# Two-layer hybrid encoder with a hierarchical MoE on one core: gate and up of each layer's first batch run together by parts, and the units that follow are loaded by parts

## The chip, the core and the metric

One core of one Trainium2 chip runs the whole program. The metric is the device time of one execution in microseconds (us). The engines that matter are TensorE (PE, with its weight loads PEld), VectorE (DVE), ScalarE (ACT), and SyncE (SP), which here only issues the DMAs that bring the weights from HBM. 16 DMA engines move the bytes.

## The reference, cut to what matters

Two layers over 256 tokens of width 1024 in float32. Each has a mixer (attention) and then a mixture of experts: 4 groups of 8 experts, the best group and its best two experts for each token.

```
for layer in range(DEPTH):                    # 2
    x = x + mixer(rmsnorm(x))                 # attention, w_in and w_out
    h = rmsnorm(x)
    pg = softmax(h @ wg + bg); g_idx = argmax(pg)
    ...                                       # top 2 of the 8 experts in the group -> comb
    for g in range(MOE_GROUPS):               # 4
        a = einsum('nd,edf->nef', h, w_gate[g])      # 8 experts, d = 1024, f = 256
        u = einsum('nd,edf->nef', h, w_up[g])
        act = silu(a) * u * comb[:, g, :, None]
        y = y + einsum('nef,efd->nd', act, w_down[g])
    x = x + y
```

## The kernel before

**Weights.** All 32 experts of a layer are loaded, 3 matrices each (gate, up, down), every matrix one *unit* of 128 partitions x 2048 floats (8 KB a partition, 1 MB). Each layer has 96 such units beside those of its mixer. A ring of 19 buffers, and 6 more that other tensors give up in the course of a layer, hold them. `place_units` fixes which buffer unit n takes (`WHERE[n]`: buffer, how many loads it has had, the unit that it replaces). SP issues the loads in the order of n: `load(n, src)` waits until PE has used the unit that lay there (`s_used`) and issues one DMA. One waiting load holds back all behind it.

**Experts.** The experts run in 8 *batches* of 4 (`batch`, on PE, ACT and DVE). Each expert takes 32 slots of the 128 columns. A batch on PE: gather the tokens of its slots (`gather`, one-hot matrices made on DVE), the gate products over the 8 chunks c of d (`rows_of(0, c)`: 4 matmuls of 256 columns, one for each expert), the up products (`rows_of(1, c)`), two transposes of the product silu(gate) * up and two of the scatter weights, the down products, and the scatter into the residual. Gate results lie in PSUM bank 4, up results in bank 0. ACT makes the silu (L1324) when gate is done, DVE multiplies it with up (L1708) when up is done. The records count two matmuls for each `pe.matmul` of float32.

**The first batch of a layer** follows the router. Before it the ring is full of weights and PE has freed nothing for a while, so nothing is left to load. It is cut finer: the tokens are gathered in four quarters (`gather_two(q)`, 2 chunks each, into the banks in `FIRST_BANK`), DVE copies each quarter out (L1659, `s_first`), and the gate products start on the first quarter. The four gate units of this batch are `PARTED`: the units that replace them (k = 25 to 28 of the layer's 96) are each loaded by three DMAs (`load_part`), of 512, 512 and 1024 columns (`PART_ENDS`: 2 KB, 2 KB and 4 KB a partition). The first two wait for `s_part`, which PE raises after chunks 0 and 1 and after chunks 2 and 3; the last waits for `s_used`. The four up units are given back together when up is done, and what replaces them (k = 29 to 32) comes in whole units.

Lines: L1048 gather matmuls of the first batch, L1056 gate and up matmuls, L1112 down, L1122 scatter, L653 a whole-unit load, L662 a load of a part.

Of the kernel before, what the change touches and what calls it, by code (L numbers as in the profile page):

```python
# [16 lines left out]
NT = SEQ // P  # L17
NC = D // P
# [8 lines left out]
DFF = 256  # L27
# [12 lines left out]
STAGE = BATCH  # L40
# [85 lines left out]
def first_unit(layer, part):  # L126
    at = 0 if layer == 0 else SLABS[0] + OUTS + PER_ROUND
    return at + {"in": 0, "out": SLABS[layer], "experts": SLABS[layer] + OUTS}[part]
# [1 line left out]

UNITS = first_unit(1, "experts") + PER_ROUND

PARTED = [first_unit(l, "experts") + j for l in range(2) for j in range(STAGE)]
PART_ENDS = (UNIT // 4, UNIT // 2, UNIT)

HALVED = [first_unit(l, "experts") + PER_ROUND - 1 for l in range(2)]
# [34 lines left out]
def hybrid_moe_kernel(nc, xT_d, small_d, bias_d, rope_d, ab_in, ab_out, c_in, c_out, gate_d, up_d, down_d, out_d):  # L171
    with ExitStack() as ctx:
# [28 lines left out]
        place = sb("place", [P, NT, 8], U32)  # L201
# [99 lines left out]
        UP_BANK = [0, 4, 3, 0]  # L301


        FIRST_BANK = [(2, 0), (3, 0), (0, 0), (2, 1)]


        Y = [6, 7, 5, 1]
# [9 lines left out]
        s_part = sem("first_parts_used")  # L317
# [85 lines left out]
        class Main:  # L403


            sig, slot = main, slot_main
# [208 lines left out]
        def _(sp):  # L615
# [39 lines left out]
            def load_part(n, src, part):  # L655
                s, _, was = WHERE[n]
                cols = slice((0, *PART_ENDS)[part], PART_ENDS[part])
                if part < len(PART_ENDS) - 1:
                    sp.wait_ge(s_part, (len(PART_ENDS) - 1) * (n >= first_unit(1, "in")) + part + 1)
                else:  # L660
                    sp.wait_ge(s_used, was + 1)
                sp.dma_start(ring_of(n)[:, cols], src[:, cols]).then_inc(s_unit[s], 16)  # L662

            for layer in range(2):
                if layer:
                    sp.wait_ge(s_used, 1 + max(n for n in range(first_unit(1, "in")) if LOW <= WHERE[n][0] < INPUT))
                    sp.dma_start(rope_all, rope_d[:, :]).then_inc(s_rope, 16)
                for s in range(layer == 0, SLABS[layer]):
                    load(first_unit(layer, "in") + s, (ab_in, c_in)[layer][s])
                    if layer == 0 and s == 2:  # L670
                        sp.dma_start(small[:, S_FIRST:S_ALL], small_d[:, S_FIRST:S_ALL]).then_inc(s_small, 16)
                        for u in extra.unit:
                            sp.sem_inc(u, 16)
                for s in range(OUTS):
                    load(first_unit(layer, "out") + s, (ab_out, c_out)[layer][s])
                weights = (gate_d, up_d, down_d)

                def expert_unit(k):
                    return weights[k % PER_BATCH // STAGE][layer, BATCH * (k // PER_BATCH) + k % STAGE]

                def load_round(rd):
                    sp.wait_ge(extra.used, EXTRA_RING * rd.turns)
                    for k in range(PER_ROUND):
                        if k >= EXTRA_RING:
                            sp.wait_ge(extra.used, EXTRA_RING * rd.turns + k - EXTRA_RING + 1)
                        e = BATCH * (k // PER_BATCH) + k % STAGE
                        sp.dma_start(low[k % EXTRA_RING][:, :], weights[k % PER_BATCH // STAGE][layer, e])\
                            .then_inc(extra.unit[k % EXTRA_RING], 16)

                for k in range(PER_ROUND):  # L690
                    if k == PER_BATCH * BEFORE_EXTRA:
                        extra_rounds(sp, layer, load_round, [(u, 16 * PER_ROUND // EXTRA_RING) for u in extra.unit])
                    n = first_unit(layer, "experts") + k
                    if WHERE[n][2] in PARTED:
                        if WHERE[n][2] == first_unit(layer, "experts"):
                            for part in range(len(PART_ENDS)):
                                for j in range(STAGE):
                                    load_part(n + j, expert_unit(k + j), part)
                        continue
                    load(n, expert_unit(k))  # L700
# [42 lines left out]
        def _(pe):  # L743
# [278 lines left out]
            def batch(rd, step, place):  # L1022
# [15 lines left out]
                    if t == NT - 1:  # L1038
                        ins.then_inc(sig.gather_ps, 1)

                def gather_two(q, *tiles):
                    for t in tiles or range(NT):
                        if q == 0:
                            pe.wait_ge(sig.onehot, NT * g + t + 1)
                        b, half = FIRST_BANK[q]
                        for c in range(2):
                            at = (2 * q + c) * P
                            ins = pe.matmul(bank2(b, 4)[:, 2 * half + c, :], tokens[:, t, at:at + P], onehot[:, t, :],  # L1048
                                            start=(t == 0 and c == 0), stop=(t == NT - 1), skip_group_check=True)
                    if t == NT - 1:  # L1050
                        ins.then_inc(s_first_ps, 1)

                def rows_of(stage, c):
                    for j in range(BATCH):
                        w = rd.weights(place, stage, j).rearrange("p (c n) -> p c n", c=NC)
                        ins = pe.matmul(bank((4, 0)[stage])[j * SLOTS:(j + 1) * SLOTS, 0:DFF],  # L1056
                                        gathered[:, c, j * SLOTS:(j + 1) * SLOTS], w[:, c, :],
                                        start=(c == 0), stop=(c == NC - 1))
                    return ins

                first = sig is main and place == 0
                if first:
                    gather_two(0)
                    gather_two(1, 0)
                else:
                    for half, t in ((0, 0), (0, 1), (1, 0), (1, 1)):
                        gather(half, t)
# [1 line left out]
                after(pe, sig.scatter, g)  # L1069
                after(pe, sig.hidden, g)  # L1070
                rd.arrived(pe, step, place, 0)
                for c in range(NC):
                    if first and c % 2 == 0:
                        pe.wait_ge(s_first, 4 * rd.layer + c // 2 + 1)
                    elif c % 4 == 0:
                        pe.wait_ge(sig.gather, 2 * g + c // 4 + 1)
                    ins = rows_of(0, c)
                    if first and (c + 1) * DFF in PART_ENDS[:-1]:
                        ins.then_inc(s_part, 1)
                    if first and c == 1:  # L1080
                        gather_two(1, 1)
                        gather_two(2)
                    elif first and c == 3:
                        gather_two(3)
                ins.then_inc(sig.used, STAGE)
                if first:
                    pe.sem_inc(sig.gather_ps, 2)
                if not last:
                    rd.arrived(pe, step, place, 1)
                    for c in range(NC):  # L1090
                        ins = rows_of(1, c)
                    ins.then_inc(sig.used, STAGE)

                if last:
                    turn_scatter(rd.layer, g)
# [719 lines left out]
```

## Time and profile before

| | |
|---|---|
| median of 3 runs | 640.93 us (640.05 to 643.5) |
| profiled execution, its span | 639.0 us |
| PE busy | 571.4 us (89%) |
| moved by DMA | 233.60 MB, mean 366 GB/s |

The span is that of one profiled execution from its first instruction to its last, 1.9 us below the median of the timed runs; the profile gives no other time for that execution. A PE that is busy 89% of the time does not mean that PE sets the time everywhere: the page shows the DMA engines at nine tenths and more in about two thirds of the slices.

### The profile page before, as it was taken

The numbers are of one execution on the slowest core, as the hardware profiler recorded it, in microseconds if no ns is written. First come the engines' busy times: TensorE is split into PE (matmuls) and PEld (weight loads), VectorE is DVE, ScalarE is ACT, GpSimd is POOL, SyncE is SP. The second block draws the span as 40 slices with busy tenths as digits, with TensorE's granted clock in tenths as the row PEclk, the third lists the DMA queues.
The fourth block names the chain that finished last, engine by engine and source line by source line (L and its number), as shares of the span: only waits on it lengthen the run. The fifth ranks groups of instructions, "written<-read, shape, count | busy, mean of one in ns | idle before, by whom it ended". The sixth has DMA issues, their size and how long they took to land.

```text
span 639.0 us, 12022 instructions
## 1 busy us (share of the span) xinstructions
PE 571.4 (89%) x4984; PEld 410.2 (64%) x4984; DVE 215.8 (34%) x723; ACT 139.6 (22%) x359; POOL 6.1 (1%) x25
## 2 busy tenths in 40 slices
PE   8999999999999698676999999999999968868696
PEld 8888776885566365352768876788556636535273
DVE  4243446163232122020426687406323212202041
ACT  3143455231101000000131366613110100000011
POOL 0100000000000000000010000000000000000000
PEclk9999999999999989797999999999999998969799
DMA  8999946579999999999999992456999999999994
GB/s 327 422 419 420 419 143 232 222 275 349 422 419 421 417 421 419 421 420 422 419 417 419 419 421 112 196 198 267 346 421 420 421 418 419 419 422 421 421 421 193
DMA packets 36782, 233.60 MB, mean 366 GB/s; under 512 B 4080, under 2 KB 4208, under 8 KB 10608
## 3 DMA queue, kind: packets, MB, share of 16 engines
q1 hardware_dynamic: 34992, 227.49, 87.4%
q10 hardware_dynamic: 1728, 5.24, 2.2%
q8 instruction: 44, 0.72, 0.5%
q14 instruction: 18, 0.15, 0.1%
HBM read 231.67 MB, written 1.05 MB: 364 GB/s over the span
## 4 chain that ended last, share of the span: by engine, by line
PE 67%; DMA 20%; SPq 6%; DVE 4%; ACT 2%; issue 1%; DVEq 0%; ACTq 0%
PE banks L786 14%; PE banks L1056 12%; DMA xT<-in_moe_w_up 9%; DMA ring<-in_moe_w_down 9%; PE banks L872 7%; PE banks L1112 7%; SPq L653 5%; PE banks L1122 5%; PE banks L1035 4%; PE banks L832 2%; PE banks L849 2%; PE banks L860 2%; DMA ring<-in_ab_w_in 2%; PE banks L996 1%; PE banks L986 1%
## 5 line engine op out<-in xcount | busy, mean ns | idle before, releaser
L1056 PE MATMUL banks<-ring,desk 128*32 128x256 f32 x1472 | 111.8, 383 | 16.1 <-DMA xT<-in_moe_w_up 9.0
L786 PE MATMUL banks<-ring,hT 128*128 128x256 f32 x416 | 94.6, 382 | 0.1
L1056 PEld LDWEIGHTS banks<-ring,desk 128*32 128x32 f32 x1472 | 59.5, 110 | 46.6 <-issue 20.4
L786 PEld LDWEIGHTS banks<-ring,hT 128*128 128x128 f32 x416 | 77.3, 190 | 13.3 <-issue 3.6
L1112 PE MATMUL banks<-ring,desk 128*32 128x512 f32 x384 | 60.3, 691 | 21.7 <-DMA ring<-in_moe_w_down 10.2
L1035 PE MATMUL banks<-desk,hT 128*128 128x128 f32 x448 | 55.7, 285 | 10.4 <-issue 10.4
L1035 PEld LDWEIGHTS banks<-desk,hT 128*128 128x128 f32 x448 | 55.3, 202 | 11.8 <-issue 11.2
L872 PE MATMUL banks<-heads,ring 128*128 128x256 f32 x256 | 61.9, 387 | 0.1
L872 PEld LDWEIGHTS banks<-heads,ring 128*128 128x128 f32 x256 | 46.4, 190 | 12.6 <-issue 6.9
L1056 PE MATMUL banks<-shared,desk 128*32 128x256 f32 x288 | 53.9, 408 | 0.0
L1122 PEld LDWEIGHTS banks<-desk 128*128 128x128 f32 x224 | 41.4, 190 | 17.0 <-issue 11.9
L1122 PE MATMUL banks<-desk 128*128 128x256 f32 x224 | 52.1, 386 | 0.0
L1112 PEld LDWEIGHTS banks<-ring,desk 128*32 128x32 f32 x384 | 15.3, 124 | 56.9 <-issue 49.8
L1324 ACT ACTIVATE desk<-banks 128x256 f32<-128x256 f32 x16 | 6.1, 384 | 184.6 <-PE banks L1056 184.6
L1667 DVE TENSOR_TENSOR desk<-banks,small 128x512 f32<-128x512 f32 x28 | 19.4, 692 | 76.1 <-PE banks L1035 76.1
L1710 DVE COPY desk<-banks 128x512 f32<-128x512 f32 x14 | 9.7, 692 | 92.9 <-PE banks L1112 92.9
L1708 DVE TENSOR_TENSOR desk<-banks,desk 128x256 f32<-128x256 f32 x14 | 5.9, 425 | 84.0 <-PE banks L1056 84.0
L1056 PEld LDWEIGHTS banks<-shared,desk 128*32 128x32 f32 x288 | 25.4, 117 | 8.1
L1112 PE MATMUL banks<-shared,desk 128*32 128x512 f32 x48 | 25.8, 687 | 0.0
L1056 PE MATMUL banks<-xT,desk 128*32 128x256 f32 x96 | 25.1, 422 | 0.0
L1523 DVE CUSTOM_DVE_ANT_0 shared<-banks,desk 128x256 f32<-128x256 f32 x32 | 12.6, 423 | 35.1 <-PE banks L832 27.8
L1329 ACT ACTIVATE desk<-banks 128x256 f32<-128x256 f32 x14 | 5.4, 384 | 76.0 <-PE banks L1103 76.0
(191 smaller groups left out, 655.6 us busy)
## 6 DMA issues: line engine op xcount, KB each, us to landing
ring<-in_moe_w_down SPq DMA_DIRECT2D x54, 1024.0 KB, 27.0
ring<-in_moe_w_gate SPq DMA_DIRECT2D x46, 1024.0 KB, 26.9
ring<-in_moe_w_up SPq DMA_DIRECT2D x46, 1024.0 KB, 26.9
shared<-in_moe_w_up SPq DMA_DIRECT2D x10, 1024.0 KB, 20.2
ring<-in_ab_w_in SPq DMA_DIRECT2D x8, 1024.0 KB, 18.7
shared<-in_moe_w_gate SPq DMA_DIRECT2D x8, 1024.0 KB, 15.0
xT<-in_moe_w_up SPq DMA_DIRECT2D x6, 1024.0 KB, 22.3
shared<-in_moe_w_down SPq DMA_DIRECT2D x6, 1024.0 KB, 26.3
```

What stands on the lines that cost most here:

```text
L653: sp.dma_start(ring_of(n), src).then_inc(s_unit[s], 16)
L786: ins = pe.matmul(bank2(SLAB_BANK[layer][s], NT)[:, t, :], hT[:, c, t * P:(t + 1) * P], w[:, c, :], start=(c == 0 and t == 0), stop=(c == ...
L832: ins = pe.matmul(bank2(r, NT)[:, t, :], heads[rows, i, t * P:(t + 1) * P], keysT[rows, kt, :], start=(t == 0), stop=True, skip_group_chec ...
L849: ins = pe.transpose(bank2(2 + r, NT)[:, c, t * P:(t + 1) * P], prob[:, r, t, c * P:(c + 1) * P], ident)
L860: ins = pe.matmul(bank(4)[r * HD:(r + 1) * HD, 0:SEQ], values[layer][:, c, cols[r]:cols[r] + HD], probT_of(layer, i)[:, r, c, :], start=(c ...
L872: ins = pe.matmul(bank2(Y[cp], 2)[:, c % 2, :], w[:, k % 2, c * P:(c + 1) * P], attT[:, k, :], start=False, stop=(k == PAIRS - 1 and c % 2 ...
L1035: ins = pe.matmul(bank(2 + half)[:, c * P:(c + 1) * P], tokens[:, t, half * HALF + c * P:half * HALF + (c + 1) * P], onehot[:, t, :], star ...
L1056: ins = pe.matmul(bank((4, 0)[stage])[j * SLOTS:(j + 1) * SLOTS, 0:DFF], gathered[:, c, j * SLOTS:(j + 1) * SLOTS], w[:, c, :], start=(c = ...
L1112: ins = pe.matmul(bank(2 + half)[j * SLOTS:(j + 1) * SLOTS, :], hiddenT[:, k, j * SLOTS:(j + 1) * SLOTS], w[:, k, half * HALF:(half + 1) * ...
L1122: ins = pe.matmul(bank2(Y[c // 2], 2)[:, c % 2, :], outputs[:, c * P:(c + 1) * P], scatter, start=False, stop=(c % 2 == 1), skip_group_che ...
L1523: ins = V.tensor_tensor_reduce(score[:, b, t, :], bank2(b, NT)[:, t, :], bias[:, b, t, :], 1.0, 3.0e38, ALU.add, ALU.min, negmax[:, b, t:t ...
L1667: V.tensor_tensor(gathered[:, 4 * h:4 * h + 4, :], bank2(2 + h, 4), gains[:, 2 * rd.layer + 1, 4 * h:4 * h + 4].unsqueeze(2) .to_broadcast ...
```

## The change

The first batch of each layer runs on PE by parts: chunks 0 and 1 of gate, then of up; then a gather; chunks 2 and 3 of gate, then of up; a gather; chunks 4 to 7 of gate, then of up. Both tiles of the second quarter are now gathered ahead of the first gate product. `s_part` is raised after each of gate and up. Eight units instead of four are `PARTED`, so k = 25 to 32 are each loaded by three DMAs, in the order: first part of all eight, second part of all eight, last part of all eight. Two quarters of the gathered tokens get other places in PSUM, since bank 0 now holds up results.

```diff
-PARTED = [first_unit(l, "experts") + j for l in range(2) for j in range(STAGE)]
+PARTED = [first_unit(l, "experts") + j for l in range(2) for j in range(2 * STAGE)]
...
-        FIRST_BANK = [(2, 0), (3, 0), (0, 0), (2, 1)]
+        FIRST_BANK = [(2, 0), (3, 0), (2, 1), (3, 1)]
...
-                    sp.wait_ge(s_part, (len(PART_ENDS) - 1) * (n >= first_unit(1, "in")) + part + 1)
+                    layer, stage = int(n >= first_unit(1, "in")), PARTED.index(was) // STAGE % 2
+                    sp.wait_ge(s_part, 2 * ((len(PART_ENDS) - 1) * layer + part) + stage + 1)
...
                             for part in range(len(PART_ENDS)):
-                                for j in range(STAGE):
+                                for j in range(2 * STAGE):
                                     load_part(n + j, expert_unit(k + j), part)
...
                 if first:
                     gather_two(0)
-                    gather_two(1, 0)
+                    gather_two(1)
...
-                for c in range(NC):
-                    if first and c % 2 == 0:
-                        pe.wait_ge(s_first, 4 * rd.layer + c // 2 + 1)
-                    elif c % 4 == 0:
-                        pe.wait_ge(sig.gather, 2 * g + c // 4 + 1)
-                    ins = rows_of(0, c)
-                    if first and (c + 1) * DFF in PART_ENDS[:-1]:
-                        ins.then_inc(s_part, 1)
-                    if first and c == 1:
-                        gather_two(1, 1)
-                        gather_two(2)
-                    elif first and c == 3:
-                        gather_two(3)
-                ins.then_inc(sig.used, STAGE)
                 if first:
+                    rd.arrived(pe, step, place, 1)
+                    for part, (begin_c, end_c) in enumerate(((0, 2), (2, 4), (4, NC))):
+                        for stage in range(2):
+                            for c in range(begin_c, end_c):
+                                if stage == 0 and c % 2 == 0:
+                                    pe.wait_ge(s_first, 4 * rd.layer + c // 2 + 1)
+                                ins = rows_of(stage, c)
+                            if part < len(PART_ENDS) - 1:
+                                ins.then_inc(s_part, 1)
+                            else:
+                                ins.then_inc(sig.used, STAGE)
+                        if part < len(PART_ENDS) - 1:
+                            gather_two(2 + part)
                     pe.sem_inc(sig.gather_ps, 2)
```

PE at the first batch of layer 0, before: the gather (L1048) of the first quarter and half of the second, then gate (L1056) and gathers in turn, and up in one piece at the end. In brackets stand the semaphores that a row waits for; `first_inputs_ready` is a quarter that DVE has copied out.

```order
L1048 MATMUL banks<-desk,hT 128x128 x3
L1056 MATMUL banks<-ring,desk 32x256 [waits unit_loaded15,unit_loaded16,unit_loaded14,first_inputs_ready,unit_loaded13,largest_count_ready]
L1056 MATMUL banks<-ring,desk 32x256 x7
L1048 MATMUL banks<-desk,hT 128x128 x6
L1056 MATMUL banks<-ring,desk 32x256 [waits first_inputs_ready]
...
L1048 MATMUL banks<-desk,hT 128x128 x4
L1056 MATMUL banks<-ring,desk 32x256 [waits first_inputs_ready]
...
L1056 MATMUL banks<-ring,desk 32x256 [waits unit_loaded0,unit_loaded1,unit_loaded18,unit_loaded17]
L1056 MATMUL banks<-ring,desk 32x256 x31
```

The same place in the changed kernel, whose lines stand one further down:

```order
L1049 MATMUL banks<-desk,hT 128x128 x5
L1057 MATMUL banks<-ring,desk 32x256 [waits unit_loaded17,unit_loaded18,unit_loaded16,unit_loaded0,unit_loaded15,unit_loaded1,unit_loaded14,first_inputs_ready,unit_loaded13,largest_count_ready]
L1057 MATMUL banks<-ring,desk 32x256 x15
L1049 MATMUL banks<-desk,hT 128x128 x4
L1057 MATMUL banks<-ring,desk 32x256 [waits first_inputs_ready]
L1057 MATMUL banks<-ring,desk 32x256 x15
L1049 MATMUL banks<-desk,hT 128x128 x4
L1057 MATMUL banks<-ring,desk 32x256 [waits first_inputs_ready]
...
L1057 MATMUL banks<-ring,desk 32x256 [waits first_inputs_ready]
L1057 MATMUL banks<-ring,desk 32x256 x23
```

The number of matmuls is the same. Two gather matmuls moved ahead of the first gate product, each run of gate products is followed by one of up products, and gate is complete 8 + 8 matmuls later in the row than before.

SP's queue behind the last load that doesn't need the first batch, before:

```order
L653 DMA shared<-in_moe_w_gate 128x2048 [waits logits_in_psum]
L662 DMA ring<-in_moe_w_gate 128x512 [waits first_parts_used] x3
L662 DMA ring<-in_moe_w_up 128x512 [waits first_parts_used]
L662 DMA ring<-in_moe_w_gate 128x512 [waits first_parts_used] x3
L662 DMA ring<-in_moe_w_up 128x512 [waits first_parts_used]
L662 DMA ring<-in_moe_w_gate 128x1024 [waits units_used] x3
L662 DMA ring<-in_moe_w_up 128x1024 [waits units_used]
L653 DMA ring<-in_moe_w_up 128x2048 [waits units_used] x3
L653 DMA ring<-in_moe_w_down 128x2048 [waits units_used] x4
```

And in the changed kernel:

```order
L653 DMA shared<-in_moe_w_gate 128x2048 [waits logits_in_psum]
L663 DMA ring<-in_moe_w_gate 128x512 [waits first_parts_used] x3
L663 DMA ring<-in_moe_w_up 128x512 [waits first_parts_used] x4
L663 DMA ring<-in_moe_w_down 128x512 [waits first_parts_used]
L663 DMA ring<-in_moe_w_gate 128x512 [waits first_parts_used] x3
L663 DMA ring<-in_moe_w_up 128x512 [waits first_parts_used] x4
L663 DMA ring<-in_moe_w_down 128x512 [waits first_parts_used]
L663 DMA ring<-in_moe_w_gate 128x1024 [waits units_used] x3
L663 DMA ring<-in_moe_w_up 128x1024 [waits units_used] x4
L663 DMA ring<-in_moe_w_down 128x1024 [waits units_used]
L653 DMA ring<-in_moe_w_down 128x2048 [waits units_used] x3
```

Where 12 DMAs of parts and 4 of whole units brought the same 8 MB, 24 DMAs of parts do. It is the same in layer 1.

## Rows read from the trace of the kernel before

**Rows 1.** The page, span in 40 slices: DMA busy tenths and rate.

```profile
DMA  8999946579999999999999992456999999999994
GB/s 327 422 419 420 419 143 232 222 275 349 422 419 421 417 421 419 421 420 422 419 417 419 419 421 112 196 198 267 346 421 420 421 418 419 419 422 421 421 421 193
```

**Rows 2.** Chain that ended last: start us, us, what.

```profile
229.06 28.30 DMA xT<-in_moe_w_up
...
270.09 27.04 DMA ring<-in_moe_w_down
...
529.27 31.41 DMA xT<-in_moe_w_up
...
570.56 29.86 DMA ring<-in_moe_w_down
```

**Rows 3.** Timeline of the first batch of layer 0, all engines.

```profile
140.81 0.42 DVE L1659 TENSOR_TENSOR desk<-banks,small 128x256 f32<-128x256 f32 x1 [0.54 <-PE banks L1048]
141.38 1.07 PE L1056 MATMUL banks<-ring,desk 128*32 128x256 f32 x16 [0.16 <-DVE desk L1659]
142.39 1.60 PE L1048 MATMUL banks<-desk,hT 128*128 128x128 f32 x12
142.51 1.28 SPq L662 DMA_DIRECT2D ring<-in_moe_w_gate  x3
...
144.92 1.16 PE L1048 MATMUL banks<-desk,hT 128*128 128x128 f32 x8
145.05 1.28 SPq L662 DMA_DIRECT2D ring<-in_moe_w_gate  x3
146.01 5.39 PE L1056 MATMUL banks<-ring,desk 128*32 128x256 f32 x96
146.12 0.42 DVE L1659 TENSOR_TENSOR desk<-banks,small 128x256 f32<-128x256 f32 x1 [1.24 <-PE banks L1048]
...
147.85 0.43 DVE L1686 TENSOR_TENSOR desk<-desk 128x256 f32<-128x256 f32 x1
148.00 1.49 SPq L662 DMA_DIRECT2D ring<-in_moe_w_gate  x3
...
148.35 1.28 ACT L1324 ACT_TABLE_LOAD   x1 [11.31 <-DVE desk L1686]
...
151.47 0.42 DVE L1708 TENSOR_TENSOR desk<-banks,desk 128x256 f32<-128x256 f32 x1 [3.11 <-PE banks L1056]
```

**Rows 4.** Stretches: busy us of each engine, PEclk, DMA share, GB/s.

```profile
140.00:144.00 4.00, 3.84 (x43) 3.02 (x45) 1.46 (x8) 0.00 (x0) 0.00 (x0) 1.00 0.13 40
144.00:148.00 4.00, 4.00 (x64) 2.52 (x68) 2.48 (x10) 0.00 (x0) 0.00 (x0) 1.00 0.98 305
148.00:152.00 4.00, 3.45 (x65) 1.86 (x57) 0.78 (x3) 1.67 (x2) 0.00 (x0) 1.00 0.92 308
152.00:156.00 4.00, 3.53 (x32) 1.30 (x36) 0.00 (x0) 1.25 (x3) 0.00 (x0) 1.00 0.99 362
...
448.00:452.00 4.00, 4.00 (x68) 2.52 (x63) 2.44 (x8) 0.12 (x1) 0.00 (x0) 1.00 0.98 297
452.00:456.00 4.00, 3.45 (x60) 1.90 (x52) 0.42 (x1) 1.54 (x2) 0.00 (x0) 1.00 0.89 279
456.00:460.00 4.00, 3.53 (x33) 0.94 (x32) 0.00 (x0) 1.26 (x3) 0.00 (x0) 1.00 1.00 400
```

**Rows 5.** The same view of two reference stretches.

```profile
3.00:9.00 6.00, 5.79 (x29) 5.29 (x29) 1.88 (x6) 3.18 (x4) 1.10 (x5) 1.00 1.02 347
...
156.00:216.00 60.00, 56.94 (x647) 36.86 (x640) 15.84 (x43) 4.92 (x12) 0.00 (x0) 1.00 1.01 421
```

**Rows 6.** DMA packets of 3:9, of 144:148 and of 156:216 us.

```profile
DMA packets 1129, 2.08 MB, mean 347 GB/s; under 512 B 126, under 2 KB 168, under 8 KB 1129
...
DMA packets 663, 1.22 MB, mean 305 GB/s; under 512 B 74, under 2 KB 74, under 8 KB 662
...
DMA packets 3493, 25.28 MB, mean 421 GB/s; under 512 B 388, under 2 KB 388, under 8 KB 439
```

More of the change, by code:

```diff
@@ L1039, in gather, with gather_two @@
                         ins.then_inc(sig.gather_ps, 1)
-                def gather_two(q, *tiles):
-                    for t in tiles or range(NT):
+                def gather_two(q):
+                    for t in range(NT):
                         if q == 0:
@@ L1071, in batch @@
                 rd.arrived(pe, step, place, 0)
-                for c in range(NC):
-                    if first and c % 2 == 0:
-                        pe.wait_ge(s_first, 4 * rd.layer + c // 2 + 1)
-                    elif c % 4 == 0:
-                        pe.wait_ge(sig.gather, 2 * g + c // 4 + 1)
-                    ins = rows_of(0, c)
-                    if first and (c + 1) * DFF in PART_ENDS[:-1]:
-                        ins.then_inc(s_part, 1)
-                    if first and c == 1:
-                        gather_two(1, 1)
-                        gather_two(2)
-                    elif first and c == 3:
-                        gather_two(3)
-                ins.then_inc(sig.used, STAGE)
-                if first:
+                if first:
+                    rd.arrived(pe, step, place, 1)
[11 more added lines that the diff above has]
+                            gather_two(2 + part)
                     pe.sem_inc(sig.gather_ps, 2)
-                if not last:
-                    rd.arrived(pe, step, place, 1)
+                else:
                     for c in range(NC):
-                        ins = rows_of(1, c)
+                        if c % 4 == 0:
+                            pe.wait_ge(sig.gather, 2 * g + c // 4 + 1)
+                        ins = rows_of(0, c)
                     ins.then_inc(sig.used, STAGE)
+                    if not last:
+                        rd.arrived(pe, step, place, 1)
+                        for c in range(NC):
+                            ins = rows_of(1, c)
+                        ins.then_inc(sig.used, STAGE)
                 if last:
```

## Prediction

> **What bounds the kernel.** I read the page's slices first. The DMA engines are full (419 to 422 GB/s) in most slices and drop twice, around 80 to 160 us and 385 to 450 us [rows 1]. Those are the late parts of the two mixers and the routers: the buffers are full of weights that PE has not used. Then the chain of what ended last. Late in both layers' experts it runs through transfers that took 27 to 31 us from issue to landing [rows 2], several units' worth of queue at 2.5 us for a unit of 1.05 MB at 421 GB/s [rows 5]. So PE is ahead at first, and then waits for a transfer queue that has been full since the first batch (156 to 216 us at a share of 1.01 [rows 5]). The end of a layer's experts is set by when transfers start again after the router, and by how long the bytes take from there. A us lost there is a us lost at the layer's end, and the next layer's mixer starts that much later. PE, DVE or ACT time in the first batch counts only through what it releases to SP.
>
> Then the timeline of the first batch [rows 3]. The first gate products end at about 142.4, and the first part's DMA is issued at 142.51; the second part at 145.05; the last at 148.00. The rest (up units) waits for the end of up at 151.4. The stretches show what the DMA engines did with that [rows 4]: almost nothing to 143.5, then 305, 308 and 362 GB/s at shares of 0.98, 0.92 and 0.99, and full speed from 156. Layer 1 gives 297, 279 and 400. In both layers 3.90 MB moved in those 12 us, 325 GB/s. The reader is to see that the engines were nearly always *busy* there, though they moved a quarter less than usual. What is missing isn't mainly released work.
>
> Packets say why. 144 to 148 us: 663 packets in 4 us x 16 engines x 0.98, 95 ns each. 3 to 9 us, the program's start, when pieces of 2 KB a partition from two queues are waiting in number: 1129 in 6 x 16 x 1.02, 87 ns each. 156 to 216 us, whole units of 8 KB rows: 3493 in 60 x 16 x 1.01, 278 ns each [rows 5, 6]. A quarter of the bytes costs about a third of the time.
>
> **The change, part by part, for one layer.**
>
> *Start of the transfers.* gather_two(1) now stands whole ahead of the first gate products. 8 gather records took 1.16 us [rows 3], so 4 more are about 0.55 us. PE waited 0.16 us there for DVE (until 141.38), which absorbs some. The first part's DMA is issued 0.4 us later: **+0.4 us**. The DMA engines stand idle there, so nothing covers it.
>
> *Releases.* PE does the same matmuls in another order; 16 records of gate or up take 1.0 us. Worked forward from the first gate at 141.8: gate part 0 released at 142.8, up part 0 at 143.8; a gather of 1.1; gate part 1 at 145.9, up part 1 at 146.9; a gather; 32 records of gate to 149.9 and 32 of up to about 151.5. Released by 145: 2.1 MB, as before; by 147: 4.2 MB instead of 2.1; by 148: 4.2, as before; by 151: 6.3 instead of 4.2. So the early release helps where the engines had run out, at a share of 0.92 in 148 to 152 and 0.89 in 452 to 456 [rows 4]. What it can regain is the distance of the mean share, (0.98 + 0.92 + 0.99) / 3 = 0.963, from the full queue's 1.01.
>
> *Size of the pieces.* 4.2 MB that came in rows of 8 KB now come in rows of 2, 2 and 4 KB. Before, the 8.39 MB of k = 25 to 32 took 4.19 MB / 325 GB/s = 12.9 us in pieces and 4.19 / 421 = 10.0 us whole, 22.9 us. After, all 8.39 MB come in pieces. No row shows 8 MB of pieces, so I bound it.
> - Above: the rate of the same pieces today, 325 GB/s, though the engines are better fed: 25.8 us, +2.9.
> - Below: 2 KB pieces at the 347 GB/s of the start, 4 KB ones at the full 421: 12.1 + 10.0 = 22.1 us, -0.8.
> - Taken: the same pieces with full engines, 325 x 1.01 / 0.963 = 341 GB/s: 24.6 us, **+1.7 us**. It is the row from this same place, with the idle share taken out.
>
> *Hidden behind the transfers.* (a) Gate is complete near 149.9 instead of 147.9, and the last quarter is copied out near 148.2 instead of 146.1, since up products stand between the gathers. DVE's weighting (L1686) ended 1.74 us after that copy [rows 3], so it ends near 150.3. ACT waits for it, loads its table for 1.28 us, and needs 0.38 us for silu: 152.0. DVE's product (L1708) then starts some 0.6 us later than 151.47. Queued behind it are the transposes and the whole PE order of later batches. That costs nothing, because the transfers lag PE by far more: by 216 us PE has begun to wait for them. Without that cover it would be 0.6 us a layer. (b) 8 more DMA issues at 0.43 us each (1.28 for three [rows 3]) are 3.4 us of SP. The queue behind them is full then, so SP would stand anyway. All eight pieces of one part stand ahead of the next part; the waits in SP's queue are met in the order in which PE releases. (c) The up units (wait for `unit_loaded` before the first gate product) landed long ago: transfers had been idle. (d) The new PSUM places add no wait: a quarter is written after the previous one in its bank was copied out.
>
> **Sum.** +0.4 + 1.7 = +2.1 us a layer, +4.2 us for two. The profiled execution has 639.0 us, so 643.2; the timed median lies 1.9 us above that, so **645.1 us**.
>
> **Rivals.**
> - *A deep queue makes small pieces cheap (no measurable change).* [...] With 4 MB of pieces waiting they might keep the rate of the start. -0.8 + 0.4 = -0.4 us a layer, 640.1; half way to my value 642.6. For it: 347 GB/s in 3 to 9 us. Against it: two queues fed the engines there, here one. Measurement tells about 0.5%, 3.2 us, from no change. Chance with all that ends within it, 0.36.
> - *The pieces were slow because they were released in drops (faster).* If all of the 325 GB/s was shortage, the eight units come at 421: 8.39 / 421 = 19.9 us, -3.0 + 0.4 = -2.6 us a layer, **635.7**. It would need 401 GB/s or more over the 8.39 MB to gain over 0.5% (22.9 - 2.0 = 20.9 us). For it: the shares of 0.92 and 0.89. Against it: 305 and 297 GB/s at a share of 0.98. Chance 0.06.
> - *The new PE order matters too (slower).* If the transfers did not cover PE's 0.6 us a layer, 646.3. Against it: the full queue to the end of the experts. It lies within the forecast.
>
> The Trainium skill has a rule for the second rival ("DMA: Bandwidth & Descriptors", section "Why small descriptors are slow"): a fixed cost of about 3 cycles per packet beside 32 bytes a cycle. A 2 KB packet would thus cost some 5% in rate. By that, as an estimate from the page, the eight units take about 20.6 us and the time is near 637. Here the trace disagrees: 87 ns for packets of 2 KB and less against 278 ns for 8 KB ones, a loss of 18% even with the queue full [rows 5, 6].
>
> **Chances and range.** Slower as forecast 0.58 (its own range 644.2 to 648), within 0.5% 0.36, faster 0.06. All terms at their upper bound: +3.3 us a layer, 647.5. The lower end takes in most of the first rival: 641.0. The upper end is 648.
>
> **What the profile after would show.** Right: the first part's issue 0.4 us later than the gate start before; DMA share about 1.0 from 144.5 to 168 us, at 330 to 350 GB/s instead of 421 in its second half; full speed only from about 168; the chain's transfers in the same place, later by 2 us in layer 0 and 4 in layer 1. Wrong: over 373 GB/s on average in that stretch, where the change breaks even (22.9 - 0.4 = 22.5 us for 8.39 MB), or a chain that no longer runs through transfers.

## The result, and the profile after

| | before | after |
|---|---|---|
| median of 20 timed runs | 641.25 us (640.05 to 644.51) | 642.43 us (641.57 to 645.24) |
| profiled execution, its span | 639.0 us | 643.3 us |
| ratio after / before | | 1.0021, 95% interval 1.0013 to 1.0030 |

The change costs 0.8 to 1.9 us in 641. It is slower, but by 0.21%, less than the 0.5% which the prediction called no change. The forecast was +4.2 us: right in sign, about three times too large. The profiled execution of the changed kernel took 645.24 us, the slowest of its twenty and 2.8 us above their median, so spans of its profile overstate the change.

The page of the changed kernel, slices of the span, with the DMA engines' tenths and rate:

```profile
DMA  8999936568999999999999993456999999999994
GB/s 328 423 420 419 411 136 219 220 282 297 415 420 420 418 419 421 420 422 419 420 417 420 421 421 128 197 193 266 341 416 419 421 419 421 420 421 421 421 420 174
...
DMA packets 39086, 233.60 MB, mean 363 GB/s; under 512 B 4336, under 2 KB 4464, under 8 KB 13936
```

The bytes, the dips and the full stretches stand where they stood in [rows 1]. Only the slice with the first batch of layer 0 is clearly lower (297 instead of 349), in part because everything there comes later in this execution. The chain of what ended last still ends both layers' experts in transfers of 27 to 30 us, as in [rows 2]; start us, us, what:

```profile
232.16 27.89 DMA xT<-in_moe_w_up
...
260.05 30.28 DMA ring<-in_moe_w_up
...
566.95 28.15 DMA ring<-in_moe_w_up
...
605.71 26.62 DMA ring<-in_moe_w_down
```

So the path is the same one. The first batch, timeline of layer 0, which answers to [rows 3]:

```profile
141.41 2.10 PE L1049 MATMUL banks<-desk,hT 128*128 128x128 f32 x16 [0.40 <-DVE desk L1655]
...
143.43 1.93 PE L1057 MATMUL banks<-ring,desk 128*32 128x256 f32 x32
...
144.56 2.47 SPq L663 DMA_DIRECT2D ring<-in_moe_w_gate  x3
...
147.08 1.87 SPq L663 DMA_DIRECT2D ring<-in_moe_w_up  x4
...
149.34 3.66 PE L1057 MATMUL banks<-ring,desk 128*32 128x256 f32 x64
...
149.47 1.63 SPq L663 DMA_DIRECT2D ring<-in_moe_w_gate  x3
...
151.67 1.28 ACT L1330 ACT_TABLE_LOAD   x1 [12.80 <-DVE desk L1692]
...
153.45 0.42 DVE L1714 TENSOR_TENSOR desk<-banks,desk 128x256 f32<-128x256 f32 x1 [1.78 <-ACT desk L1330]
...
154.30 1.60 SPq L663 DMA_DIRECT2D ring<-in_moe_w_gate  x3
```

The same first gather in the timeline of the kernel before:

```profile
139.57 1.65 PE L1048 MATMUL banks<-desk,hT 128*128 128x128 f32 x12 [0.40 <-DVE desk L1649]
```

The profiled execution of after is already 1.84 us later at this point (141.41 against 139.57). No edit touches anything ahead of it, so I take that off. From first gather to first issue: 3.15 us here; before, 142.51 - 139.57 = 2.94.

The load queue on SP in layer 1, from the first piece on (start us, us, what):

```profile
449.33 1.28 SPq L663 DMA_DIRECT2D ring<-in_moe_w_gate  x3
450.65 1.85 SPq L663 DMA_DIRECT2D ring<-in_moe_w_up  x4
452.55 0.43 SPq L663 DMA_DIRECT2D ring<-in_moe_w_down  x1
453.02 1.81 SPq L663 DMA_DIRECT2D ring<-in_moe_w_gate  x3
454.88 2.65 SPq L663 DMA_DIRECT2D ring<-in_moe_w_up  x4
457.58 0.46 SPq L663 DMA_DIRECT2D ring<-in_moe_w_down  x1
458.08 2.63 SPq L663 DMA_DIRECT2D ring<-in_moe_w_gate  x3
```

Here is something that the order of the program doesn't tell. The last parts of gate's replacements are issued 8.75 us after the first piece (458.08 - 449.33). Before it was 5.49 us (148.00 - 142.51 in [rows 3]; 5.50 in layer 1). The sixteen pieces ahead of them took SP 8.7 us. So SP, and not PE, sets when they are issued: in layer 0 gate was done near 151.2, by an estimate (half of the 64 records from 149.34), and its last parts were issued at 154.30. Stretches of 4 us (columns as in [rows 4]):

```profile
144.00:148.00 4.00, 4.00 (x68) 2.44 (x59) 1.11 (x6) 0.00 (x0) 0.00 (x0) 1.00 0.47 145
148.00:152.00 4.00, 4.00 (x68) 2.60 (x64) 2.04 (x7) 0.33 (x1) 0.00 (x0) 1.00 0.81 259
152.00:156.00 4.00, 2.60 (x36) 1.11 (x32) 0.42 (x1) 1.99 (x4) 0.00 (x0) 1.00 0.97 302
156.00:160.00 4.00, 4.00 (x34) 1.83 (x27) 1.20 (x4) 0.60 (x1) 0.00 (x0) 1.00 1.05 405
160.00:164.00 4.00, 4.00 (x28) 3.72 (x28) 0.59 (x3) 0.00 (x0) 0.00 (x0) 1.00 1.03 407
164.00:168.00 4.00, 4.00 (x58) 3.05 (x60) 2.70 (x7) 0.00 (x0) 0.00 (x0) 1.00 1.02 410
168.00:172.00 4.00, 4.00 (x80) 2.42 (x76) 0.21 (x2) 0.38 (x1) 0.00 (x0) 1.00 1.05 424
...
448.00:452.00 4.00, 4.00 (x59) 2.53 (x61) 1.57 (x7) 0.00 (x0) 0.00 (x0) 1.00 0.38 120
452.00:456.00 4.00, 4.00 (x65) 2.56 (x60) 1.60 (x6) 0.00 (x0) 0.00 (x0) 1.00 0.86 263
456.00:460.00 4.00, 2.57 (x44) 1.35 (x36) 0.86 (x3) 2.26 (x4) 0.00 (x0) 1.00 1.00 338
460.00:464.00 4.00, 4.00 (x35) 1.31 (x29) 0.45 (x1) 0.67 (x2) 0.00 (x0) 1.00 1.05 403
```

Two things stand against my reading. Pieces of 2 and 4 KB a partition are carried at 403 to 410 GB/s once the queue holds many. And the start is slow though bytes are there: by 454.83 SP had issued 11 pieces of layer 1 (2.9 MB), and by 456 the engines had moved (120 + 263) x 4 = 1.5 MB.

In one figure: from first issue until 8.39 MB had moved (bytes of 1 us stretches added up) took 23.8 and 23.9 us before (layers 0 and 1) and 25.1 and 24.1 after. That is 1.3 and 0.2 us, with 0.2 us of later issue in each layer 1.9 us in all, against a measured 0.8 to 1.9. In layer 0, where most of it lies, SP's first three issues took 2.47 us instead of 1.28, and all that stands behind them is issued later; layer 1 has no such issue and lost 0.2. One profile alone is good to about 1 us a layer, so the verdicts below go by timed medians. Every experiment was timed beside the kernel before on the same chip; that one's medians were 641.1 to 641.5.

### The profile page after: what moved, and what is told of

Same layout as the page of the kernel before. It is cut to its first block, busy times and chain, and to the rows that moved or that the text cites. A ratio compares the mean times of both kernels' runs of the same rounds, so it can differ in the third digit from the quotient of the medians.

```text
span 643.3 us, 12038 instructions
## 1 busy us (share of the span) xinstructions
PE 574.4 (89%) x4984; PEld 412.4 (64%) x4984; DVE 216.4 (34%) x723; ACT 139.4 (22%) x359; POOL 6.1 (1%) x25
## 3 DMA queue, kind: packets, MB, share of 16 engines
HBM read 231.67 MB, written 1.05 MB: 362 GB/s over the span
## 4 chain that ended last, share of the span: by engine, by line
PE 63%; DMA 23%; SPq 4%; DVE 4%; ACT 2%; issue 2%; DVEq 0%; ACTq 0%
PE banks L787 14%; PE banks L1057 11%; DMA ring<-in_moe_w_up 9%; DMA ring<-in_moe_w_down 8%; PE banks L873 7%; PE banks L1118 5%; PE banks L1036 5%; PE banks L1128 5%; SPq L653 4%; DMA xT<-in_moe_w_up 4%; PE banks L762 3%; PE banks L833 2%; PE banks L861 2%; PE banks L850 2%; PE banks L1049 1%
## 5 line engine op out<-in xcount | busy, mean ns | idle before, releaser
L1057 PE MATMUL banks<-ring,desk 128*32 128x256 f32 x1472 | 115.7, 397 | 18.9 <-DMA xT<-in_moe_w_up 9.6
L1118 PE MATMUL banks<-ring,desk 128*32 128x512 f32 x384 | 56.9, 655 | 18.3 <-DMA shared<-in_moe_w_down 7.6
L1118 PE MATMUL banks<-shared,desk 128*32 128x512 f32 x48 | 24.6, 662 | 0.0
```

The costliest lines, as they stand in the source:

```text
L1118: ins = pe.matmul(bank(2 + half)[j * SLOTS:(j + 1) * SLOTS, :], hiddenT[:, k, j * SLOTS:(j + 1) * SLOTS], w[:, k, half * HALF:(half + 1) * ...
```

## The experiments

### The two halves of the change

**order alone.** PE runs the changed order; gate's replacements come in parts as before, up's come whole when up is done.

```diff
-PARTED = [first_unit(l, "experts") + j for l in range(2) for j in range(2 * STAGE)]
+PARTED = [first_unit(l, "experts") + j for l in range(2) for j in range(STAGE)]
...
-                                for j in range(2 * STAGE):
+                                for j in range(STAGE):
```

> The changed order on TensorE, but the units that replace up come whole after up is done, as before. Yardstick: from the first gather of a layer's experts to that layer's end, 190.8 and 190.9 us before, 192.1 and 192.1 us in the changed kernel. Theory A (the loss is the size of the pieces): the stretch is at most 0.3 us above before (the 0.2 us by which the first part is issued later), and the time 641.7 or less beside 641.3. Theory B (the loss is the new order: later start, later silu, later release of gate's last part): the stretch stays near 192, and the time near 642.4. Gate's last part is released 2 us later here with nothing given for it, so B may even give more, 643.

**pieces alone.** PE runs the old order; up's replacements come in three parts, all of them after up is done.

```diff
...
-                if part < len(PART_ENDS) - 1:
+                if part < len(PART_ENDS) - 1 and PARTED.index(was) // STAGE % 2 == 0:
...
-                            for part in range(len(PART_ENDS)):
-                                for j in range(STAGE):
+                            for stage in range(2):
+                                for part in range(len(PART_ENDS)):
+                                    for j in range(STAGE * stage, STAGE * (stage + 1)):
```

> The old order on TensorE and the old releases, but the four units that replace up come in pieces of 512, 512 and 1024 columns, all after up is done. Theory A (size of the pieces): the second 4.19 MB cost as much as the first, up to +1.4 us a layer, time 643 to 644. Theory B (order): no more than 0.2 us a layer, time within 0.5 us of before. What the trace of the changed kernel shows speaks for B here: once the queue was full, its 2 KB and 4 KB pieces moved at 405 to 410 GB/s against 421 to 425 for whole units, so 4.19 MB cost 0.3 to 0.4 us more, two layers 0.7 us.

Measured: order alone 644.59 us, ratio 1.0048 (1.0031 to 1.0065), about +3.1 us. Pieces alone 641.97 us, ratio 1.0011 (1.0001 to 1.0021), about +0.7 us: 0.35 a layer (0.03 to 0.7 by the interval), where I had 1.7. The order costs more than the whole change does, and cutting up's units costs next to nothing when they stand at the end of a filled queue. SP in the first batch of layer 0, order alone:

```profile
142.62 2.62 SPq L663 DMA_DIRECT2D ring<-in_moe_w_gate  x3
...
145.76 1.38 SPq L663 DMA_DIRECT2D ring<-in_moe_w_gate  x3
...
149.38 1.28 SPq L663 DMA_DIRECT2D ring<-in_moe_w_gate  x3
...
151.18 2.02 SPq L653 DMA_DIRECT2D ring<-in_moe_w_up  x3
```

The second parts of gate's replacements are issued 0.7 us later than before, the last parts 1.4 us (149.38 against 148.00), and the up units no earlier. In layer 1 the last parts are 1.3 us later, counted from the first issue (6.77 us after it instead of 5.50). The order delays gate's replacements, and in the changed kernel early pieces of up stand against that.

### What a late issue costs

**no pieces.** The kernel before, with all four gate units' replacements whole.

```diff
-PARTED = [first_unit(l, "experts") + j for l in range(2) for j in range(STAGE)]
+PARTED = []
```

> The kernel before with no unit cut: k = 25 to 32 all come whole, four after gate and four after up. If release is what counts, the first transfer starts 5.4 us later (148.0 instead of 142.5), the second megabyte after that at full speed: 4.19 MB done at 149.1 + 10.0 = 159.1 instead of 156.4, 2.7 us a layer, time 646.6. If a start of transfers in whole units runs near 421 GB/s and one in pieces at 325, as before, the same. If a start is slow whatever the size (302 to 325 GB/s in its first 10 us), 4 us a layer, 649.

**late last part.** The kernel before, but the last parts of gate's replacements (2.1 MB) wait until up is done too.

```diff
-                    sp.wait_ge(s_used, was + 1)
+                    sp.wait_ge(s_used, was + 1 + STAGE)
```

> The kernel before, and only the last parts of gate's replacements (2.1 MB) wait for the end of up: 151.4 us instead of 147.9. Nothing of TensorE's order changes. If order_alone lost 3.1 us because those parts were released 2 us later, this loses at least as much: 3 to 6 us, 644 to 647. If it lost them through the later silu and the rest of the order, this one stays within 1 us of before.

Measured: no pieces 647.33 us, 1.0088 (1.0071 to 1.0104), +5.6 us for a first issue 5.5 us later in each layer (8.43 us after the first gather instead of 2.94). Late last part 646.43 us, 1.0079 (1.0057 to 1.0102), +5.1 us, where those parts were issued 8.95 us after the first piece instead of 5.49:

```profile
142.04 1.28 SPq L662 DMA_DIRECT2D ring<-in_moe_w_gate  x3
...
150.99 1.28 SPq L662 DMA_DIRECT2D ring<-in_moe_w_gate  x3
```

Its stretches:

```profile
148.00:152.00 4.00, 3.45 (x60) 1.92 (x52) 0.42 (x1) 1.54 (x2) 0.00 (x0) 1.00 0.53 188
152.00:156.00 4.00, 3.53 (x34) 0.94 (x32) 0.00 (x0) 1.26 (x3) 0.00 (x0) 1.00 0.91 237
```

The share falls to 0.53: the queue runs dry. That is 2.5 us a layer for 3.5 us of lateness (the up units behind those parts wait too). By the same price the 1.3 to 1.5 us of lateness in order alone are worth 0.9 to 1.1 of its 1.5 us a layer, an estimate. So the late gate parts explain most of what the order costs; the rest may be the first issue 0.2 us later and the second parts 0.4 to 0.7 us later, which no run separates.

No pieces shows another side. Its whole units, into a queue just as empty:

```profile
147.65 1.28 SPq L653 DMA_DIRECT2D ring<-in_moe_w_gate  x3
```


```profile
148.00:152.00 4.00, 3.45 (x64) 1.97 (x52) 0.42 (x1) 1.66 (x2) 0.00 (x0) 1.00 0.86 279
152.00:156.00 4.00, 3.53 (x35) 0.95 (x33) 0.00 (x0) 1.25 (x3) 0.00 (x0) 1.00 1.02 430
156.00:160.00 4.00, 4.00 (x22) 3.30 (x19) 1.78 (x5) 0.00 (x0) 0.00 (x0) 1.00 1.01 428
```

They run at 430 GB/s within 5 us. The pieces of [rows 4] needed 12. The start as such isn't slow. These units differ from the pieces in three things, though: the number of DMAs, the length of the rows, and that 7 MB were issued within 5 us. Merged pieces below holds rows and releases fixed.

### The price of small rows in a full queue

**deep pieces.** The kernel before, and 16 later units of each layer (k = 36 to 51, 33.6 MB in all) each in four DMAs of 512 columns.

```diff
...
+QUARTERED = [first_unit(l, "experts") + k for l in range(2) for k in range(36, 52)]
...
+                if n in QUARTERED:
+                    for k in range(4):
+                        part = slice(k * UNIT // 4, (k + 1) * UNIT // 4)
+                        sp.dma_start(ring_of(n)[:, part], src[:, part]).then_inc(s_unit[s], 16)
```

> The kernel before, and 16 more units of each layer (k = 36 to 51, issued when the queue is already full) come in four pieces of 512 columns each. Prices the 2 KB piece with a full queue, 33.6 MB of it. My prediction took 341 GB/s for pieces of 2 and 4 KB together with full engines: 16.8 MB / 341 - 16.8 / 421 = +9.3 us a layer, 660. What the changed kernel's trace showed once its queue was full (405 GB/s): +1.6 us a layer, 644.4. Rate of the start (347 GB/s): +8.5 us a layer, 658. If every DMA costs 0.9 us whatever its size (the 300 GB/s that pieces show in the first 10 us), the queue runs empty: 64 x 0.9 = 57.6 us for what took 39.9, up to +17 us a layer, 670.

Measured: 650.64 us, 1.0138 (1.0110 to 1.0166), about +9 us. Stretches, then the packets of 484 to 524 us:

```profile
180.00:190.00 10.00, 10.00 (x156) 7.31 (x158) 2.91 (x8) 0.38 (x1) 0.00 (x0) 1.00 1.06 387
...
210.00:220.00 10.00, 8.10 (x56) 4.32 (x52) 2.30 (x6) 1.25 (x3) 0.00 (x0) 1.00 0.95 322
484.00:494.00 10.00, 10.00 (x88) 7.74 (x84) 3.58 (x9) 0.58 (x1) 0.00 (x0) 1.00 1.05 387
```

```profile
DMA packets 8409, 15.47 MB, mean 387 GB/s; under 512 B 937, under 2 KB 937, under 8 KB 8386
```

Nearly all packets are small, and the rate is 387 GB/s: 40 x 16 x 1.05 / 8409 = 80 ns a packet, not the 95 ns on which the prediction rests. Rows of 2 KB cost 8% of 421 in a full queue. At 387 instead of 421 GB/s, 33.6 MB take 7.0 us more; the rest of the 9 us lies where the queue ran thin (0.95, 322).

### Fewer DMAs for the same bytes

**merged pieces.** The kernel before; the first and the second parts of three neighbouring gate units come by one DMA of 128 x 3 x 512 each. Bytes, rows and waits stay, 12 DMAs of parts become 8.

```diff
...
-                sp.dma_start(ring_of(n)[:, cols], src[:, cols]).then_inc(s_unit[s], 16)
+                j = PARTED.index(was) % STAGE
+                if part < len(PART_ENDS) - 1 and j == 0:
+                    sp.dma_start(rings[:, s:s + 3, cols], src[:, :, cols].rearrange("e p n -> p e n")).then_inc(s_unit[s], 16)
+                elif part == len(PART_ENDS) - 1 or j == 3:
+                    sp.dma_start(ring_of(n)[:, cols], src[:, cols]).then_inc(s_unit[s], 16)
```

> The kernel before, with the first and second parts of the three gate units among k = 25 to 28 fetched by one DMA each of 128 x 3 x 512 (0.79 MB in 2 KB rows) instead of three of 0.26 MB. Same bytes, same row size, same release, 4 DMAs instead of 8. If a DMA's own cost (0.86 us each at 305 GB/s) makes the slow first 10 us, the rate there rises toward 387 GB/s, the full-queue rate of 2 KB rows, and 1 us or more a layer comes back: 639. If it is the rows or the engines' start, the stretch stays at 270 to 310 GB/s and the time within 0.5 us of before.

Measured: 639.54 us, 0.9977 (0.9963 to 0.9990), -1.5 us. A stretch and its packets:

```profile
144.00:148.00 4.00, 4.00 (x64) 2.52 (x63) 2.51 (x9) 0.00 (x0) 0.00 (x0) 1.00 1.00 362
```

```profile
DMA packets 732, 1.45 MB, mean 362 GB/s; under 512 B 32, under 2 KB 32, under 8 KB 731
```

Against 305 GB/s in [rows 4] and 74 packets under 512 B in [rows 6]: the small records that go with each DMA are fewer, and SP needs 0.92 us for a part of the four units instead of 1.75 (142.44 to 143.36 against 142.51 to 144.26). Which of the two counts, this run doesn't tell. Layer 1 shows the same: 2.37 MB had moved 8 us after the first issue, against 2.01 before.

**two parts.** The kernel before, gate's replacements in parts of 512 and 1536 columns: fewer DMAs, but the second part's early release is given up.

```diff
-PART_ENDS = (UNIT // 4, UNIT // 2, UNIT)
+PART_ENDS = (UNIT // 4, UNIT)
```

> The kernel before, with k = 25 to 28 in two parts of 512 and 1536 columns: 1 MB after chunk 1, the other 3.1 MB when gate is done at 147.9. The second MB is released 2.9 us later than before. late_last_part lost 5.1 us for 2.1 MB given back 3.5 us later; if it is megabytes times lateness that count, 1.05 x 2.9 against 2.1 x 3.5 gives 2.1 us, 643.4. If the engines were still busy with the first MB until 147 (1.1 MB moved by then), only 1 to 2 us of idleness follow, at most 2 us a layer, and fewer small pieces give 0.2 back. No faster than 641 by either.

Measured: 643.88 us, 1.0040 (1.0027 to 1.0053), +2.8 us. An early release is worth more than four DMAs saved; merging has both.

### The release of up

**up parts, old order.** All of gate first, then up, but up is given back by parts too.

```diff
...
+                    layer, stage = int(n >= first_unit(1, "in")), PARTED.index(was) // STAGE % 2
+                    sp.wait_ge(s_part, 4 * layer + 2 * stage + part + 1)
...
+                        if first and (c + 1) * DFF in PART_ENDS[:-1]:
+                            ins.then_inc(s_part, 1)
```

> The old order on TensorE, gate's replacements as before, and up's replacements also in three parts, the first two given back after chunks 1 and 3 of up (148.8 and 149.7 us instead of 151.4). The pieces of pieces_alone (642.0), released earlier. If released work is what is missing 6 to 11 us after the first issue (240 to 305 GB/s there), at least 0.5 us a layer comes back: 640.9, and without pieces_alone's 0.7 us 640.2. If the slow start is in the pieces or the engines, it stays near 642.

**up halves, old order.** The same with two parts of 1024 columns, `UP_ENDS = (UNIT // 2, UNIT)`.

> As up_parts_old_order, but up's replacements in two halves of 1024 columns, the first given back after chunk 3 of up (149.7 us). 4 MB in 8 DMAs instead of 12. If release counts, between 640.2 and 641; if only the number of pieces counts, 641.3 to 641.5; not above 642 by either.

Measured: 642.52 us, 1.0015 (1.0001 to 1.0029), and 642.4 us, 1.0009 (0.9993 to 1.0024). Neither gains anything, beside before or beside pieces alone (1.0011), where the same pieces of up came only after up was done.

**split gather.** The changed kernel with one tile of the second quarter gathered behind the first gate products again, as before the change.

```diff
...
-                    gather_two(1)
+                    gather_two(1, 0)
...
+                            if part == 0:
+                                gather_two(1, 1)
```

> The changed kernel, but only half of the second quarter is gathered ahead of the first gate product, as before; the rest follows behind the first up product. The first part is issued 0.2 us earlier in each layer. If the late start costs what it measures, the time is 0.4 to 0.5 us below the changed kernel (642.0); if the slow start hides it, no difference.

Measured: 641.74 us, 1.0000 (0.9988 to 1.0011): level with before. By the ratios that is about 1.3 us under the changed kernel, by the medians beside before 0.6 (+0.6 against +1.2). The earlier start accounts for 0.4 us. SP in layer 0:

```profile
142.22 1.29 SPq L663 DMA_DIRECT2D ring<-in_moe_w_gate  x3
...
150.98 1.41 SPq L663 DMA_DIRECT2D ring<-in_moe_w_gate  x3
```

From first issue until 8.39 MB had moved took 23.6 and 24.1 us here, 25.1 and 24.1 in the changed kernel. The difference is all in layer 0, where the first three issues took 1.29 us here and 2.47 there. In the two profiles the long issue fits as the cause of the rest; whether it came in most of the timed runs isn't known, so for the medians the cause stays open.

**gate before up's rest.** PE runs chunks 0 and 1 of gate, 0 and 1 of up, then all of gate, then the rest of up. Early pieces of up, and gate given back nearly as early as before.

```diff
...
-                    for part, (begin_c, end_c) in enumerate(((0, 2), (2, 4), (4, NC))):
+                    for stage, begin_c, end_c in ((0, 0, 2), (1, 0, 2), (0, 2, 4), (0, 4, NC), (1, 2, NC)):
...
-                            for part in range(len(PART_ENDS)):
-                                for j in range(2 * STAGE):
+                            for part, stage in ((0, 0), (0, 1), (1, 0), (2, 0), (1, 1), (2, 1)):
+                                for j in range(STAGE * stage, STAGE * (stage + 1)):
```

> split_gather with another order behind the second gather: chunks 2 to 7 of gate, then 2 to 7 of up, so that gate's last parts (2.1 MB) are given back 0.9 us earlier and up's second parts (1 MB) 1.9 us later. If the lateness of gate's last part is what the changed order costs (5.1 us for 3.5 us of lateness), and up's second parts arrive in a queue that is not empty, about 1 us below split_gather: 640.7 beside 641.3 of before. If the queue is not short of work there, the same as split_gather.

**merged, with early up.** The same with neighbouring units in one DMA in every part (three gate units, two up units): 15 DMAs for 8.39 MB instead of 24.

```diff
...
+TOGETHER = {0: 3, 1: 0, 2: 0, 4: 2, 5: 0}
...
+                if together(was) > 1:
+                    sp.dma_start(rings[:, s:s + together(was), cols], src[:, :, cols].rearrange("e p n -> p e n")).then_inc(s_unit[s], 16)
```

> gate_before_up_late (641.3), with neighbouring units fetched together in every part: 15 DMAs for the 24 of before, three gate units or two up units in one. Same bytes, rows and releases. merged_pieces, with 4 DMAs of parts less, gained 1.6 us. If the number of DMAs in the slow start is what ate the early release of up, this gains at least as much on gate_before_up_late: 639.7 or less, and the early release should then show on top of merged_pieces (639.5): 638.5 to 639.3. If the early release of up is worth nothing even so, 639.5 to 640.

Measured: gate before up's rest 641.27 us, 1.0002 (0.9991 to 1.0013), the same as split gather, though SP issued gate's last parts 2.0 us earlier in layer 0 (6.76 us after the first issue instead of 8.76) and 1.1 in layer 1:

```profile
149.09 1.57 SPq L663 DMA_DIRECT2D ring<-in_moe_w_gate  x3
```

So where pieces of up are queued too, the lateness of gate's last parts shows no price of its own (up's second parts came later in return); late last part has its price at a queue that ran dry. Merged, with early up 638.42 us, 0.9952 (0.9939 to 0.9966), -3.1 us, the fastest of all here and faster than both kernels. Its stretches:

```profile
144.00:148.00 4.00, 4.00 (x60) 2.57 (x62) 2.44 (x11) 0.00 (x0) 0.00 (x0) 1.00 1.02 354
148.00:152.00 4.00, 3.45 (x60) 1.92 (x52) 1.14 (x4) 1.67 (x2) 0.00 (x0) 1.00 1.01 373
152.00:156.00 4.00, 3.53 (x34) 0.94 (x32) 0.00 (x0) 1.25 (x3) 0.00 (x0) 1.00 1.04 415
```

The share is above 1.0 throughout, and from 144 to 156 the engines moved (354 + 373 + 415) x 4 = 4.6 MB; before it was 3.9, in merged pieces 4.2. Merging 24 DMAs into 15 is worth some 3 us on gate before up's rest, where merging 12 into 8 was worth 1.5 on the kernel before. Against merged pieces (0.9977) the intervals overlap a little. This run also merges the last parts and up's pieces, which merged pieces doesn't, so how much of its lead is early up and how much is fewer DMAs isn't shown.

## Why the prediction was wrong in size

*What bounds the kernel.* Right: transfers set both layers' ends, and a us lost at the restart is lost at the end. No pieces and late last part show it with their +5.6 and +5.1 us, 2.8 and 2.5 a layer: counted from the first gather of layer 0, their 8.39 MB were through 3.2 and 3.1 us later than before. PE, DVE and ACT counted only through what they release.

*Size of the pieces*, +1.7 us a layer: this term failed. Pieces alone measured 0.35. I took the rate of the first 12 us, 325 GB/s scaled to 341, as the price of rows of 2 and 4 KB. With many pieces queued, rows of 2 KB ran at 387 (deep pieces), and a mix with 4 KB at 403 to 410 (the changed kernel). The slow start belongs to many small DMAs into an empty queue: whole units reached 430 GB/s there, and three pieces in one DMA raised 305 to 362 GB/s. In the changed kernel both meet, and the eight units took 0.75 us longer a layer from first issue (1.3 and 0.2, the first with SP's long issue in it). With the two sizes measured, the prediction's own sum gives 0.2 + 0.35 = 0.55 us a layer, an estimate of +1.1 us where 0.8 to 1.9 was measured. So the term of the pieces is what put the forecast off. The bound below used 347 GB/s of the program's start, another restart, so it could not show what a full queue does either.

The rival *A deep queue makes small pieces cheap* described the measured case, at 0.36: the full queue does better than the start's 347 GB/s, though why isn't shown. I placed it at 640.1 to 642.6; 642.43 is at its upper end. The Trainium skill's rule ("DMA: Bandwidth & Descriptors", section "Why small descriptors are slow"), some 5% of rate for 2 KB packets by the estimate in the prediction, is much closer to the measured 8% than my 18%. Where I wrote that the trace disagrees, I had taken two restarts for the steady state. The time near 637 that I drew from it didn't come, since that sum gave the rule's rate to the restart as well.

*Releases.* Compared by amounts released, the list holds, but two things were missing. Gate's last parts come later, and order alone, where nothing comes early in return, lost 1.5 us a layer, most of it by them. And released isn't issued: I expected 4.2 MB by 147, 4.5 us after the first issue. In layer 1 SP had issued 4.2 MB only after 8.7 us; the kernel before had after 7.5 (142.51 to 150.00). Early pieces of up make up most of the loss: 3.1 us with the order alone, 0.8 to 1.9 with the pieces. That I had next to nothing for this step came out right by luck, as the difference of two larger terms that I had not seen.

*Hidden behind the transfers.* (b) was wrong in its reason: the eight extra issues are not behind a full queue, they stand ahead of gate's last parts while the queue fills. (a) was harmless: DVE's product began at 153.45 - 1.84 = 151.61, 0.14 us later than before, not 0.6. The rival *The new PE order matters too* meant that path; the order matters, but through the late gate parts. (c) and (d) showed no wait.

*Start of the transfers*: 0.2 us a layer, not 0.4. Split gather takes it away and gains 0.6 to 1.3 us in all.

*The pieces were slow because they were released in drops (faster)* is refuted in this form: the change releases more at a time, and the first 8 us after the first issue moved 1.72 and 1.96 MB (layers 0 and 1), against 2.17 and 2.01 before.

*What the profile would show.* Expected was a share of 1.0 from 144.5 and 330 to 350 GB/s in the second half. It was 0.47, 0.81, 0.97 first and 405 to 410 after; the first of these stretches begins 0.56 us before the first issue, and in 1 us stretches the share stood at 0.70 to 0.85 from 1 to 8 us after it (0.90 to 1.12 before). So I had the first half too fast and the second too slow. Counted from the first bytes, as I counted (about 1 us after the first issue), the eight units took some 24.1 and 23.1 us, not 24.6, against 22.9.

Open: what in a small DMA costs the time at the start, SP's 0.43 us an issue or something on the queue's side; and how much of split gather's lead over the changed kernel is more than its earlier start.

## What to carry to other kernels

When a queue restarts from empty, count DMAs as well as bytes, and try neighbouring buffers in one DMA before cutting finer; take the price of small rows from a stretch where the queue is full, never from the restart. When work is reordered to release something earlier, list what is released later in return, and when the queue's engine can really issue it.

## What was unexpected

- With many pieces queued, rows of 2 KB cost only 8% (387 against 421 GB/s, 80 ns a packet); the same rows took 95 ns just after the restart.
- Merging three pieces into one DMA, with the same rows and bytes, raised the rate after the restart from 305 to 362 GB/s in the first stretch of 4 us.
- Among SP's first issues of a layer one often takes 0.6 to 1.3 us longer: three took 2.47 and 2.62 us in layer 0 of the changed kernel and of order alone, 2.12 and 2.07 in layer 1 of pieces alone and no pieces, and 1.28 in both layers of the kernel before (there a single one took 1.50 at 146.38). In each of these traces a 16 KB packet of an instruction queue moved within a microsecond of the long issue; in the stretches of the kernel before and the changed kernel without a long issue there was none. That SP waits for its instructions there is a guess. The delay is as large as the effect measured here, so one profile can mislead about a layer.
